# The opening of an adaLN, HGRN2 and window-attention step: turns, chunks and feature blocks in another order

## What is computed

```python
ada = jax.nn.silu(c) @ w_ada + b_ada              # c: 1 prompt row + 8 sample rows; w_ada: 1024 x 3072
shift, scale, gate = jnp.split(ada, 3, axis=-1)
h = rmsnorm(x, norm_w) * (1 + scale[:, None]) + shift[:, None]
proj = h @ w_in
q, f, i, z = jnp.split(proj, ...)                 # 8 heads; q and f are 128 wide for each
```

## Time and profile before

| | |
|---|---|
| time, median of 3 runs | 1081.74 us (1081.57 to 1081.86) |
| the profiled execution's own time | 1079.47 us |
| its span, first to last instruction | 1077.7 us |
| PE busy | 1059.7 us, 98% of the span |
| DVE, ACT, POOL busy | 645.2 us (60%), 508.1 us (47%), 149.1 us (14%) |
| mean granted clock of TensorE | 0.999 of full speed |
| first matmul that is not in the opening (L467) | starts at 53.02 us |

### The profile page before, as it was taken

How to read it: one execution, slowest core, us unless ns; L and a number is a source line. 1 busy time by engine, 2 the same in 40 slices (tenths; PEclk the granted TensorE clock), 3 DMA queues, 4 the chain that set the end, 5 groups by cost and what they waited for, 6 DMA issues and landing times.

```text
span 1077.7 us, 24568 instructions
## 1 busy us (share of the span) xinstructions
PE 1059.7 (98%) x10237; PEld 974.4 (90%) x10237; DVE 645.2 (60%) x1301; ACT 508.1 (47%) x1049; POOL 149.1 (14%) x167
## 2 busy tenths in 40 slices
PE   8999999999999999999999999999999999999998
PEld 5799999999999999989998789888988998898997
DVE  4785767676768686875436744644464446347333
ACT  4653444444454545464224455545455464566122
POOL 2000010101000000000000550343035204410000
PEclk9999999999999999999999999999999999999999
DMA  9862536363536364127525454426443544444432
GB/s 322 303 198 85 175 103 179 101 175 105 176 104 177 105 177 143 35 97 246 153 86 164 111 138 127 132 63 160 128 131 91 130 129 117 113 117 111 118 104 59
DMA packets 233300, 147.80 MB, mean 137 GB/s; under 512 B 8899, under 2 KB 227229, under 8 KB 232678
## 3 DMA queue, kind: packets, MB, share of 16 engines
q1 hardware_dynamic: 218544, 134.35, 43.5%
q10 hardware_dynamic: 14646, 11.89, 3.3%
HBM read 124.19 MB, written 22.02 MB: 136 GB/s over the span
## 4 chain that ended last, share of the span: by engine, by line
PE 92%; DVE 3%; ACT 2%; SPq 1%; DMA 1%; issue 1%; POOL 0%; ACTq 0%; DVEq 0%; POOLq 0%
PE PJ L446 27%; PE PJ L1805 17%; PE PJ L1495 16%; PE PJ L467 9%; PE X L1293 2%; PE PJ L1864 1%; PE X L1352 1%; PE X L1954 1%; PE X L1473 1%; PE PJ L754 1%; PE PJ L493 1%; DMA pre<-in_ada_w_dram 1%; PE X L1920 1%; PE X L1475 1%; SPq L2691 1%; PE X L1366 1%
## 5 line engine op out<-in xcount | busy, mean ns | idle before, releaser
L446 PE MATMUL PJ<-h_hi,w_hi 128*128 128x288 f32 (+2 forms) x672 | 147.4, 301 | 0.5 <-ACT v_ L1009 0.5
L446 PE MATMUL PJ<-h_lo,w_hi 128*128 128x288 f32 (+2 forms) x672 | 143.7, 295 | 0.0
L446 PE MATMUL PJ<-h_hi,w_low 128*128 128x288 f32 x672 | 139.9, 296 | 0.0
L446 PEld LDWEIGHTS PJ<-h_hi,w_hi 128*128 128x128 f32 x672 | 108.1, 189 | 3.2 <-issue 3.0
L446 PEld LDWEIGHTS PJ<-h_lo,w_hi 128*128 128x128 f32 x672 | 108.5, 189 | 0.0
L412 ACT ACTIVATE w_hi<-raw 128x1024 fp32r<-128x1024 f32 (+1 forms) x91 | 92.7, 1035 | 32.1 <-PE PJ L1805 16.0
L446 PEld LDWEIGHTS PJ<-h_hi,w_low 128*128 128x128 f32 x672 | 106.5, 189 | 0.0
L467 PE MATMUL PJ<-w_hi,h_hi 128*128 128x256 f32 x320 | 91.1, 292 | 0.8 <-DVE q_ L1129 0.8
L419 DVE TENSOR_TENSOR w_low<-raw,w_hi 128x1024 fp32r<-128x1024 f32 x64 | 77.3, 1224 | 23.8 <-ACT w_hi L412 23.3
L467 PE MATMUL PJ<-w_low,h_hi 128*128 128x256 f32 x320 | 88.0, 283 | 0.0
L1805 PE MATMUL PJ<-w_hi,h_hi 128*128 128x512 f32 x210 | 84.7, 403 | 1.8 <-DVE w_low L419 1.8
(11 more groups left out here) (388 smaller groups left out, 2449.3 us busy)
## 6 DMA issues: line engine op xcount, KB each, us to landing
raw<-in_a_w_in_dram SPq DMA_DIRECT2D x48, 512.0 KB, 4.8
raw<-in_ada_w_dram SPq DMA_DIRECT2D x28, 512.0 KB, 3.8
kvc<-in_cache_kv_w_dram SPq DMA_DIRECT2D x24, 512.0 KB, 5.1
pre<-in_ada_w_dram SPq DMA_DIRECT2D x16, 512.0 KB, 9.9
s<-in_state_hgrn_dram SPq DMA_DIRECT2D x8, 1024.0 KB, 8.3
out_hgrn_sample_dram<-s ACTq DMA_DIRECT2D x8, 1024.0 KB, 5.2
raw<-in_a_w_out_dram SPq DMA_DIRECT2D x16, 512.0 KB, 4.8
raw<-in_b_w_in_dram SPq DMA_DIRECT2D x64, 128.0 KB, 2.3
```

What stands on the lines that cost most here:

```text
L446: last = nc.tensor.matmul(PJ[:, 2 * s + e, 0:n1 - n0], a[:, k, :], b[:, k, n0:n1], start=(k == 0 and i == 0), stop=(k == KD - 1 and i == 2))
```

## The change

Four things move in the opening; no arithmetic of the result and no transfer is added or taken away.

1. `first_ada(0)` goes from behind the turn of x block 5 to behind block 7. The turns of blocks 6 and 7 and `first_norm_pe(1)` now come ahead of it.
2. `turn_ada` of chunk 0 goes ahead of `first_ada(1)`; on DVE, `scale_x(0)` and `scale_x(1)` go ahead of the copy of chunk 2's rows.
3. `first_ada(2)` (chunk 1) goes from behind block 0 to ahead of block 0, behind the matmuls of ones, of which two are taken out. Its row copy on ACT goes from behind block 3 to behind block 1, and its turn stands behind block 1. `first_ada(3)` (chunk 3) goes from behind block 1 to behind block 2, its turn from there to behind block 3.
4. Blocks 6 and 7 are no longer done as block 6 for q and f, block 7 for q and f, but as both blocks for q and then both for f.

```diff
@@ first_pe
                 if k == 6:
                     first_norm_pe(1)
-                if k == 5:
-                    pe.wait_ge(c_sb, 1)
-                    pe.wait_ge(par_done, 1)
-                    first_ada(0)
+            pe.wait_ge(c_sb, 1)
+            pe.wait_ge(par_done, 1)
+            first_ada(0)
             first_norm_pe(2)
             first_norm_pe(3)
             first_norm_pe(4)
             pe.wait_ge(s_fold, 16)
+            turn_ada(adr0[:, 0], 0, ada_t0[:, 0:4])
             pe.wait_ge(x_sb, KD)
             first_ada(1)
-            turn_ada(adr0[:, 0], 0, ada_t0[:, 0:4])
             turn_ada(adr0[:, 2], 1, ada_t0[:, 8:12])
-            for _ in range(12):
+            for _ in range(10):
                 pe.matmul(X[:, 2, 0:P], ones[:], ones[:], start=True, stop=True)
-            for k in range(KD):
-                first_tickets(pe, k)
-                if k == 0:
-                    first_ada(2)
+            first_ada(2)
+            for k in range(KD - 2):
+                first_tickets(pe, k, range(2))
                 if k == 1:
+                    turn_ada(adr0[:, 1], 2, ada_t0[:, 4:8])
+                if k == 2:
                     pe.wait_ge(n_r, 1)
                     first_ada(3)
-                    turn_ada(adr0[:, 1], 2, ada_t0[:, 4:8])
+                if k == 3:
                     turn_ada(adr0[:, 3], 3, ada_t0[:, 12:16])
+            for t in range(2):
+                for k in range(KD - 2, KD):
+                    first_tickets(pe, k, (t,))
@@ first_tickets
-            for t in range(2):
+            for t in tickets:
@@ first_act, behind the high part of block k
+                if k == 1:
+                    first_ada_rows(act, 2, copy)
                 if k == 3:
-                    first_ada_rows(act, 2, copy)
                     first_ada_rows(act, 3, copy)
@@ first_dve
-            first_ada_rows(dve, 1, dve.tensor_copy)
             scale_x(0)
             scale_x(1)
+            first_ada_rows(dve, 1, dve.tensor_copy)
             amplitudes(0)
```

More of the change, by code:

```diff
@@ L728, in first_pe, with first_tickets @@
             pe.wait_ge(s_fold, 16)
+            turn_ada(adr0[:, 0], 0, ada_t0[:, 0:4])
             pe.wait_ge(x_sb, KD)
             first_ada(1)
-            turn_ada(adr0[:, 0], 0, ada_t0[:, 0:4])
             turn_ada(adr0[:, 2], 1, ada_t0[:, 8:12])
-            for _ in range(12):
+            for _ in range(10):
                 pe.matmul(X[:, 2, 0:P], ones[:], ones[:], start=True, stop=True)
-            for k in range(KD):
-                first_tickets(pe, k)
-                if k == 0:
-                    first_ada(2)
+            first_ada(2)
+            for k in range(KD - 2):
+                first_tickets(pe, k, range(2))
                 if k == 1:
+                    turn_ada(adr0[:, 1], 2, ada_t0[:, 4:8])
+                if k == 2:
                     pe.wait_ge(n_r, 1)
                     first_ada(3)
-                    turn_ada(adr0[:, 1], 2, ada_t0[:, 4:8])
+                if k == 3:
                     turn_ada(adr0[:, 3], 3, ada_t0[:, 12:16])
-        def first_tickets(pe, k):
+            for t in range(2):
+                for k in range(KD - 2, KD):
+                    first_tickets(pe, k, (t,))
+        def first_tickets(pe, k, tickets):
             pe.wait_ge(n_hx, k + 1)
             pe.wait_ge(n_lo, k + 1)
-            for t in range(2):
+            for t in tickets:
                 pe.wait_ge(raw_split, t + 1)
```

## The result

The changed kernel takes 1086.39 us (median of 4 runs, 1085.97 to 1087.24) against 1081.74: 4.65 us more by the medians, or 0.43%. The ratio of the runs on record, 1.0053 with an interval of 1.0041 to 1.0064, is larger and makes 5.7 us (4.4 to 6.9). The forecast was 1083.84, +2.10: the direction was right, the size far too small. What I had put down as rival 1, the fall of the clock, is what happened.

A forecast was written before the change was run, and what follows sets the result against it. PE was taken to bound the kernel, with the opening's shift going through to the end: +2.75 for the later turn less 0.65 for the tickets, +2.10, made 1083.84 us, slower by 0.19%, range 1081.8 to 1086.6.

The forecast's parts named there:

- rival 1: PE's gap before block 4: the clock falls to half over the four last blocks; 1085.3 to 1086.8 us, chance 0.36.
- part 3: Chunks among the blocks: last turn 2.75 us later, PE idle about 3.6 us, then the four last blocks as before.
- The turn later by 2.75: PE's opening: the last turn ends at 44.68 us in place of 41.93, with blocks 0, 2 and 3 ahead of it.
- The idle behind it: PE behind the last turn: idle about 3.6 us in place of 0.38, block 4 starting near 48.35.
- Part 4: Blocks 6 and 7 ticket by ticket: q complete sooner, winning 0.65 of PE's 0.80 us idle before the first product.
- The sum of the order alone: First product after the opening: +2.75 for the later turn less 0.65 for the tickets, +2.10 us, chance 0.48.
- Rival 1's price: Four last blocks on PE: one slow start costs 1.47 us, from 24 records of ones taking 4.39 and later 2.92.
- Parts 1 and 2: Opening, first_ada(0) behind all turns of x and chunk 0's turn ahead of first_ada(1): worth nothing on the path.
- The early chunk 1: PE's opening: chunk 1's product starts at 32.35 in place of 34.49 us, giving 2.14 us back.
- The two matmuls of ones: Opening: taking them out, 0.24 us each, only lengthens PE's wait for chunk 1.
- Rival 2: Opening in timed runs: chunk 3 lands after 40.2 us, so the new order costs only +0.1, 1081.9 us; chance 0.11.
- Rival 3: Opening: faster, 0.65 us from the tickets if the last turn stayed at 41.93; chance 0.05 with anything overlooked.

The follow-up runs named there:

- e3: The changed kernel with blocks 6 and 7 done for q and f together again; 1.0055 times the kernel before (1.0036 to 1.0074).
- e5: The changed kernel with 4 more matmuls of ones in the gap behind the last turn; 1086.67 us, 1.0057 times the kernel before.
- e6: The changed kernel unaltered, profiled and timed a second time; 1086.63 us against 1080.83 for the kernel before, ratio 1.0054.
- e1: The changed kernel with 14 more matmuls of ones filling the gap behind the last turn; 1083.20 us, 1.0021 times the kernel before.
- e2: The changed kernel with chunk 3's product and both turns put back behind block 1; 1081.12 us, 1.0006 times the kernel before.
- e4: The kernel before with only blocks 6 and 7 done both for q, then both for f; 1079.24 us against 1081.15, ratio 0.9991.
- e7: The kernel before with chunk 3 and the turns placed as in the change and 14 matmuls of ones in the gap; ratio 1.0030.
- e8: The kernel of e4 with DVE's and ACT's waits for the last turn filled with work; 1079.09 us against 1080.83 before, ratio 0.9990.
- e11: The kernel before with 10 matmuls of ones in the opening in place of 12, nothing else; 1.0013 times the kernel before.
- e10: The kernel of e4 with 10 matmuls of ones in the opening in place of 12; 1.0012 times the kernel before.
- e9: The kernel of e2 with 12 matmuls of ones in the opening in place of 10; 1.0001 times the kernel before.
- e12: The changed kernel with 12 matmuls of ones in the opening in place of 10; 1085.8 us, 1.0047 times the kernel before.

## Why the prediction was wrong

**The step that failed is the one in part 3 that ends with the gap**: "The four last blocks follow as before." I had the gap (3.6 us forecast, 3.66 measured), and I had the row that showed a clock falling after 2.1 us, and still costed the blocks behind the gap at full clock, with the fall as a rival at 0.36. In all four profiles with a gap of over 2.6 us and an undisturbed opening (changed, e3, e5, e6) the clock fell; in none with the gap filled or under 0.5 us (e1, e2, e4, e7, e8) did it fall in the opening. It belonged in the sum. Why the clock falls at one place in one execution and at another in the next stays open.

**The terms.** The turn later by 2.75: measured 2.50, since chunk 1's product started at 32.23 and not 32.35, and a turn takes 0.8 to the next operation where I had 0.98. The idle behind it: right. Part 4, 0.65: right (e4). The sum of the order alone, +2.10: the changed kernel's opening without the clock's part is 2.51 - 0.64 = 1.87 later, e1's 1.5 to 2.0, and e1's timed 2.3 holds a wait near 470 us besides. Rival 1's price, 1.47 from one slow start: 1.4 to 2.3 measured; the row gave the lower end, but by luck as far as the rows say, since the view of the granted clock has 1.00 over those first microseconds and doesn't show that start as slow by the clock. With 2.33 in the sum, 2.51 - 0.64 + 2.33 = 4.20 is the shift to the first product. The timed 4.65 is near it, the 5.7 of the ratio is not: the waits near 470 us can make up the difference.

**What was hidden.** Parts 1 and 2 are worth nothing, as said: e2 and e4 reach the first product at 52.14 and 52.16. The early chunk 1 too, in the good order, as chunk 3's landing then holds PE; in the changed order it gives 0.5 to 0.8 (e7 against e1).

**A cost I had at nothing.** The two matmuls of ones. In the opening they are idle work, and the wait for chunk 1 covers them. But without them PE waits 2.0 to 2.3 us near 470 us (the profiles of e11 and e10). How much of that is in the 4.65 stays open, since the timed runs of before may have had these waits as well; in the runs of e9 to e12 it is a loss of 2.2 by the medians of e11 and before (1082.31 and 1080.08), and of 1.4 (0.2 to 2.5) by their ratio.

**The other rivals.** Rival 2 didn't come: chunk 3 was never waited for in the changed order. Rival 3: no cause appeared.

The Trainium skill's rule that I weighed, in "TensorE: Matmul & The Clock Gate", section on HAM oscillation (a long wait between bursts lets the array fall to half rate, and the next burst starts cold), describes what these traces show, 0.50 of the clock from 46.9 to 53.7. A fall within a gap of 2.7 us, another behind a wait of 1.84 (both e5) and one only behind a gap of 3.7 us (e6) show that the length of the gap alone doesn't fix the place.

## What to carry to other kernels

Put the work on which the other engines' long chain hangs (here the last turn) ahead of PE work that is ready anyhow, and keep that ready work behind it as cover: two blocks moved from behind the turn to ahead of it cost 3.0 us with the clock kept up. Where a move opens a gap on PE in front of dense work, put the half clock into the sum, and fill the gap: in this kernel gaps of 2.67 and 3.66 us cost 1.4 to 2.3 us each time, and waits of 1.6 to 1.8 us brought a fall twice and none in other places. And compare starts of named instructions in two profiles before whole times: waits of 2 us far behind the change can hide or double its effect.

## What was not expected of the hardware

- The clock fell 1.2 us behind PE's last matmul in one execution (gap 2.7 us, e5), 2.4 us behind it in another (gap 3.7 us), and in three it held through a 3.7 us gap and fell 0.2 to 0.5 us into the next burst (e6, e3, e12). It fell behind a wait of 1.84 us (e5, 472 us) and not behind one of 1.8 us (L1805 in the profile of before). At half clock a matmul of 288 columns went at 0.24 us in place of 0.13.
- Two matmuls fewer at 29 us brought waits of PE at 468 and 472 us (1.0 and 0.9 us; 2.5 us more from L446 to the end), beside a later arrival of the program's own instructions. That the late instructions make PE wait is what the two views suggest; why the count decides wasn't tried further.
